# One wide product per weight tile in the feed-forward's first layer: 512 columns into a whole bank, the two half sums added by ScalarE and VectorE

## The reference, cut to what matters

```python
D_MODEL, SEQ, FFN_DIM, CONV_WIDTH = 1024, 256, 2752, 3

def conv_glu_ffn(h, w_in, conv_w, conv_b, w_out):
    S = h.shape[1]
    u = h @ w_in                                   # (256 x 1024) @ (1024 x 5504)
    up = jnp.pad(u, ((0, 0), (CONV_WIDTH - 1, 0), (0, 0)))
    c = conv_b
    for tap in range(CONV_WIDTH):
        c = c + up[:, tap:tap + S] * conv_w[tap]   # a causal filter of 3 taps along the tokens
    gate, val = c[..., :FFN_DIM], c[..., FFN_DIM:]
    return (jax.nn.silu(gate) * val) @ w_out       # (256 x 2752) @ (2752 x 1024)

# per layer:  x = x + attention(rmsnorm(x));  x = x + conv_glu_ffn(rmsnorm(x), ...)
```

## Time and profile before

| | us |
|---|---|
| median of 3 runs | 723.19 (720.53 to 723.85) |
| the profiled execution, its own time | 723.07 |
| its span in the profile | 721.3 |
| the two feed-forward loops within it | about 207 to 376 and 531 to 702 |

### The profile page before, as it was taken

One profiled execution on the slowest core, in us unless ns is written; L12 is line 12 of the kernel. 1 busy time (PEld: TensorE's weight loads), 2 busy tenths in 40 slices (PEclk: granted clock), 3 DMA queues, 4 the chain that ended last, 5 costly groups with the idle time before them and its releaser, 6 DMA issues.

```text
span 721.3 us, 11799 instructions
## 1 busy us (share of the span) xinstructions
PE 670.7 (93%) x4196; PEld 583.9 (81%) x4196; DVE 490.5 (68%) x922; ACT 394.9 (55%) x767; POOL 33.7 (5%) x61
## 2 busy tenths in 40 slices
PE   5999896999989999999999999787989999999995
PEld 4998565666889999999997788655889999999994
DVE  4387469684587777766678555685687777766675
ACT  5454334663585555555556455363685555555554
POOL 0200034000000000000000100302000000000000
PEclk9999998999999999999999999989999999999998
DMA  7465053000626544445541554420536545555521
GB/s 265 159 212 182 27 206 116 2 1 1 217 107 241 196 176 175 175 178 191 202 187 59 192 175 169 165 88 1 203 121 240 187 181 179 175 177 186 200 79 58
DMA packets 19614, 109.10 MB, mean 151 GB/s; under 512 B 2432, under 2 KB 2816, under 8 KB 10240
## 3 DMA queue, kind: packets, MB, share of 16 engines
q1 hardware_dynamic: 19584, 108.71, 41.9%
HBM read 107.65 MB, written 1.05 MB: 151 GB/s over the span
## 4 chain that ended last, share of the span: by engine, by line
PE 78%; DVE 12%; ACT 5%; DMA 2%; issue 2%; POOL 1%; SPq 0%; POOLq 0%; DVEq 0%; ACTq 0%
PE psA L356 11%; PE psA L357 11%; PE psA L358 11%; PE psT L452 6%; PE psO L454 6%; PE psO L453 6%; PE psO L452 6%; PE psT L454 6%; PE psT L453 6%; PE psO L641 2%; PE psO L617 2%; DVE stat L1461 2%; DMA stage<-in_w_group 2%; DVE win_lo L1227 2%; DVE arena L1495 1%
## 5 line engine op out<-in xcount | busy, mean ns | idle before, releaser
L1308 DVE TENSOR_TENSOR win_lo<-stage,win_hi 128x1024 fp32r<-128x1024 f32 x90 | 109.4, 1219 | 5.7 <-ACT win_hi L926 5.7
L1324 DVE SCALAR_TENSOR_TENSOR arena<-psO,prm,arena 128x255 f32<-128x255 f32 x84 | 40.1, 478 | 90.8 <-ACT arena L944 90.8
L926 ACT ACTIVATE win_hi<-stage 128x1024 fp32r<-128x1024 f32 x92 | 96.0, 1050 | 6.4 <-PE psA L358 6.4
L452 PE MATMUL psT<-hA_hi,win_hi 128*128 128x256 f32 x336 | 95.2, 283 | 1.7 <-DVE hA_lo L1243 1.7
L453 PE MATMUL psO<-hA_lo,win_hi 128*128 128x256 f32 x336 | 95.2, 283 | 0.0
L452 PE MATMUL psO<-hA_hi,win_hi 128*128 128x256 f32 x336 | 95.2, 283 | 0.0
L454 PE MATMUL psT<-hA_hi,win_lo 128*128 128x256 f32 x336 | 95.2, 283 | 0.0
L454 PE MATMUL psO<-hA_hi,win_lo 128*128 128x256 f32 x336 | 95.2, 283 | 0.0
L453 PE MATMUL psT<-hA_lo,win_hi 128*128 128x256 f32 x336 | 95.2, 283 | 0.0
L1227 DVE TENSOR_TENSOR win_lo<-stage,win_hi 128x1024 fp32r<-128x1024 f32 (+3 forms) x56 | 62.3, 1152 | 32.2 <-ACT win_hi L874 31.9
L944 ACT ACTIVATE arena<-psO,prm 128x256 f32<-128x256 f32 x42 | 23.7, 563 | 89.7 <-PE psO L454 89.7
(11 more groups left out here) (242 smaller groups left out, 1358.9 us busy)
## 6 DMA issues: line engine op xcount, KB each, us to landing
stage<-in_w_ffn_in SPq DMA_DIRECT2D x44, 1024.0 KB, 5.4
stage_out<-in_w_ffn_out SPq DMA_DIRECT2D x44, 516.0 KB, 3.5
stage<-in_w_kv SPq DMA_DIRECT2D x8, 1024.0 KB, 4.8
stage<-in_w_group SPq DMA_DIRECT2D x5, 1024.0 KB, 5.1
stage<-in_w_phi SPq DMA_DIRECT2D x4, 1024.0 KB, 4.9
stage<-in_w_nsa_out SPq DMA_DIRECT2D x4, 1024.0 KB, 5.0
stage<-in_w_dq SPq DMA_DIRECT2D x4, 1024.0 KB, 4.8
stage<-in_w_dout SPq DMA_DIRECT2D x4, 1024.0 KB, 4.8
```

Of the source, the lines that this page charges most:

```text
L452: mm(o, win_hi[:, slot, cs], hA_hi[:, k, :], start=k == 0, stop=False)
L926: act.activation(win_hi[:, slot, h * W // 2:(h + 1) * W // 2], stage[:, slot, h * W // 2:(h + 1) * W // 2], ACT.Copy).then_inc(sem["in_hi" ...
L1308: last = dve.tensor_tensor(win_lo[:, slot, cs], stage[:, slot, cs], win_hi[:, slot, cs].bitcast(F32), sub)
L1324: dve.scalar_tensor_tensor(conv[:, b, g, k:S], (psT, psO)[g][:, b, 0:S - k], prm[:, b, 4 * g + 2 - k:4 * g + 3 - k], conv[:, b, g, k:S], A ...
```

## The change

High and low half of the normalised tokens now lie side by side: one tile `hA` of [128, 8, 2, 256], of which `hA_hi` and `hA_lo` are views. `up` makes one product of 512 columns with the high weights (both halves as the moving operand, into a whole bank of 512) and one of 256 with the low weights, added to the first 256 columns of the bank. So u is in the bank as two sums: columns 0 to 255 hold high by high plus low by high, columns 256 to 511 hold high by low. ScalarE copies the second half into `u_part` in SBUF, and VectorE adds it to the first half of the bank and writes `u_sum`. The filter then reads `u_sum` instead of the bank, on both engines. VectorE now takes the gate's two taps first and then the value's, and copies the parameters ahead of the value's taps. ScalarE's first half split of `win` now stands between the copy and the filter of g = 1. TensorE's waits on `gate2` and `val2` become waits on `u_sum`.

```diff
--- before
+++ after
@@ tiles @@
-        hA_hi = sb("hA_hi", [P, KT, S], F32R)
-        hA_lo = sb("hA_lo", [P, KT, S], F32R)
+        hA = sb("hA", [P, KT, 2, S], F32R)
+        hA_hi, hA_lo = hA[:, :, 0, :], hA[:, :, 1, :]
+        u_part = arena[:, 4096:4608].rearrange("p (g q) -> p g q", g=2)
+        u_sum = arena[:, 4608:5120].rearrange("p (g q) -> p g q", g=2)
@@ TensorE, up(); up_last() in the same way @@
-                            o = (psT, psO)[g][:, b, 0:S]
-                            mm(o, win_hi[:, slot, cs], hA_hi[:, k, :], start=k == 0, stop=False)
-                            mm(o, win_hi[:, slot, cs], hA_lo[:, k, :], start=False, stop=False)
-                            last = mm(o, win_lo[:, slot, cs], hA_hi[:, k, :], start=False, stop=k == KT - 1)
+                            o = (psT, psO)[g][:, b, :]
+                            mm(o, win_hi[:, slot, cs], hA[:, k, :, :].rearrange("p a q -> p (a q)"), start=k == 0, stop=False)
+                            last = mm(o[:, 0:S], win_lo[:, slot, cs], hA_hi[:, k, :], start=False, stop=k == KT - 1)
@@ TensorE, the loop @@
-                        pe_.wait_ge(sem["val2"], 2 * i + (f0 + b + 1))
-                        pe_.wait_ge(sem["gate2"], 2 * i + (f0 + b + 1))
+                        pe_.wait_ge(sem["u_sum"], 4 * i + (2 * f0 + 2 * b + 2))
@@ ScalarE, step() @@
-                        act.activation(conv[:, b, g, :], (psT, psO)[g][:, b, 0:S], ACT.Identity,
+                        act.activation(u_part[:, g, :], (psT, psO)[g][:, b, S:2 * S], ACT.Copy).then_inc(sem["u_part"], 1)
+                        if g == 1 and split_next:
+                            split_in(j + 2, b, 0)
+                        act.wait_ge(sem["u_sum"], 2 * j + (2 * f0 + g + 1))
+                        act.activation(conv[:, b, g, :], u_sum[:, g, :], ACT.Identity,
                                        bias=prm[:, b, 4 * g + 3:4 * g + 4], scale=prm[:, b, 4 * g + 2:4 * g + 3]).then_inc(sem["conv0"], 1)
-                    if split_next:
-                        split_in(j + 2, b, 0)
@@ ScalarE, last_step() @@
-                    act.activation(conv[:, 1, 0, :], psT[:, 1, 0:S], ACT.Identity, bias=prm[:, 1, 3:4], scale=prm[:, 1, 2:3]).then_inc(sem["conv0"], 2)
+                    act.activation(u_part[:, 0, :], psT[:, 1, S:2 * S], ACT.Copy).then_inc(sem["u_part"], 2)
+                    act.wait_ge(sem["u_sum"], 2 * (f0 + NJ))
+                    act.activation(conv[:, 1, 0, :], u_sum[:, 0, :], ACT.Identity, bias=prm[:, 1, 3:4], scale=prm[:, 1, 2:3]).then_inc(sem["conv0"], 2)
@@ VectorE @@
+                def add_parts(j, b, g):
+                    dve.wait_ge(sem["u_part"], 2 * j + (2 * f0 + g + 1))
+                    dve.tensor_tensor(u_sum[:, g, :], (psT, psO)[g][:, b, 0:S], u_part[:, g, :], ALU.add).then_inc(sem["u_sum"], 1)
@@ VectorE, last_step() @@
+                    dve.wait_ge(sem["u_part"], 2 * (f0 + NJ))
+                    dve.tensor_tensor(u_sum[:, 0, :], psT[:, 1, 0:S], u_part[:, 0, :], ALU.add).then_inc(sem["u_sum"], 2)
+                    dve.wait_ge(sem["u_sum"], 2 * (f0 + NJ))
```

More of the change, by code:

```diff
@@ L106 @@
 scores smax negmax probs recip factor scaled_p pT_bank pT_act pT_dve oT_bank oT_hi oT_lo
-x_new u_bank conv0 gate1 val1 gate2 val2 silu prod a_hi a_lo
+x_new u_bank u_part u_sum conv0 gate1 val1 gate2 val2 silu prod a_hi a_lo
 dk_bank dk_act dk_dve dq_bank dq_act dq_dve
@@ L463, in up_last @@
                     pe_.wait_ge(sem["in_lo"], first + NJ)
-                    pe_.wait_ge(sem["gate2"], f0 + NJ - 2)
+                    pe_.wait_ge(sem["u_sum"], 2 * (f0 + NJ - 2))
                     for k in range(KT):
                         cs = slice(k * P, (k + 1) * P)
[L468 to L471, removed]
+                        o = psT[:, 1, :]
+                        before = mm(o, win_hi[:, slot, cs], hA[:, k, :, :].rearrange("p a q -> p (a q)"), start=k == 0, stop=False)
+                        last = mm(o[:, 0:S], win_lo[:, slot, cs], hA_hi[:, k, :], start=False, stop=k == KT - 1)
                     before.then_inc(sem["u_bank"], 1)
@@ L493, in ffn @@
                     for b in range(2):
-                        pe_.wait_ge(sem["val2"], 2 * i + (f0 + b + 1))
-                        pe_.wait_ge(sem["gate2"], 2 * i + (f0 + b + 1))
+                        pe_.wait_ge(sem["u_sum"], 4 * i + (2 * f0 + 2 * b + 2))
                         up(2 * i + (2 + b), b)
                         down(2 * i + (1 + b), 1 - b, False, False)
-                pe_.wait_ge(sem["val2"], f0 + NJ - 3)
-                pe_.wait_ge(sem["gate2"], f0 + NJ - 3)
+                pe_.wait_ge(sem["u_sum"], 2 * (f0 + NJ - 3))
                 up(NJ - 2, 0)
@@ L1323, in tap @@
                     wait()
-                    dve.scalar_tensor_tensor(conv[:, b, g, k:S], (psT, psO)[g][:, b, 0:S - k], prm[:, b, 4 * g + 2 - k:4 * g + 3 - k],
+                    dve.scalar_tensor_tensor(conv[:, b, g, k:S], u_sum[:, g, 0:S - k], prm[:, b, 4 * g + 2 - k:4 * g + 3 - k],
                                              conv[:, b, g, k:S], ALU.mult, ALU.add).then_inc(sem[done], 1)
+                def add_parts(j, b, g):
+                    dve.wait_ge(sem["u_part"], 2 * j + (2 * f0 + g + 1))
+                    dve.tensor_tensor(u_sum[:, g, :], (psT, psO)[g][:, b, 0:S], u_part[:, g, :], ALU.add).then_inc(sem["u_sum"], 1)
                 def step(j, b, split_next=True, split_wout=True):
+                    add_parts(j, b, 0)
                     tap(b, 0, 1, lambda: dve.wait_ge(sem["conv0"], 2 * j + (2 * f0 + 1)), "gate1")
+                    tap(b, 0, 2, lambda: dve.wait_ge(sem["gate1"], j + (f0 + 1)), "gate2")
+                    add_parts(j, b, 1)
+                    take_params(j + 1, 1 - b)
                     tap(b, 1, 1, lambda: dve.wait_ge(sem["conv0"], 2 * j + (2 * f0 + 2)), "val1")
-                    tap(b, 0, 2, lambda: dve.wait_ge(sem["gate1"], j + (f0 + 1)), "gate2")
                     tap(b, 1, 2, lambda: dve.wait_ge(sem["val1"], j + (f0 + 1)), "val2")
-                    take_params(j + 1, 1 - b)
                     if split_next:
@@ L1346, in last_step @@
                     taps = [prm[:, 1, k:k + 1] for k in range(2)]
+                    dve.wait_ge(sem["u_part"], 2 * (f0 + NJ))
+                    dve.tensor_tensor(u_sum[:, 0, :], psT[:, 1, 0:S], u_part[:, 0, :], ALU.add).then_inc(sem["u_sum"], 2)
+                    dve.wait_ge(sem["u_sum"], 2 * (f0 + NJ))
                     for k, done in ((1, "gate1"), (2, "gate2")):
                         dve.wait_ge(sem["conv0" if k == 1 else "gate1"], 2 * (f0 + NJ) if k == 1 else f0 + NJ)
-                        dve.scalar_tensor_tensor(conv[:, 1, 0, k:S], psT[:, 1, 0:S - k], taps[2 - k], conv[:, 1, 0, k:S],
+                        dve.scalar_tensor_tensor(conv[:, 1, 0, k:S], u_sum[:, 0, 0:S - k], taps[2 - k], conv[:, 1, 0, k:S],
                                                  ALU.mult, ALU.add).then_inc(sem[done], 1)
```

## The result

The changed kernel takes 723.98 us (median of 20 runs, 722.34 to 725.47) against 722.74 us before (20 runs, 720.53 to 723.94). The ratio is 1.0018, with a 95% interval of 1.0009 to 1.0026: slower by about 1.2 us. It lies within the 0.5% that was called "same" and within the range, but on the other side of no change than the forecast of 721.5.

The account below looks back on a forecast made before the run. TensorE was taken to bound the loop, at 8.30 us a group against VectorE's 8.22. The terms: 723.07 - 7.6 + 2 x 1.15 + 2.5 + 1.2 = 721.5 us, range 718.8 to 729.0.

Parts of the forecast that it names:

- What bounds the loop, the chain, its price: Feed-forward loop: TensorE sets the period at 8.30 us; VectorE's chain through ScalarE takes 8.09 to 8.22, 8.22 taken.
- The start term: Start of each layer: the first down waits for the longer elementwise chain of the first groups, +1.15 us a layer.
- The end terms: End of each layer: the last down waits for VectorE's longer chain, +2.5 us in layer 0, +1.2 in layer 1.
- The product term: Up in the loop: one product less per weight tile saves 13.6 ns a pair, 0.20 us a group, 7.6 in all.
- the clean stream: A down that no up precedes: 512-column products take 0.2264 us each, giving 0.346 a pair and 0.22 saved a group.
- The first: Loop: VectorE's chain exceeds 8.30 us and sets the period; 729 us at a chain of 8.40; chance 0.25.
- The second: Loop, starts and ends: VectorE's chain is only 8.01 us, so starts and ends cost less; 719.3 us; chance 0.15.
- The third: Up: the wide product pays back its saved cost; 727 us at 2.5 ns a product, 723 at 8 ns; chance 0.08.
- the fourth: Layer 0's last down: TensorE's clock falls in the 2.8 us gap, products take 0.427 us, 723.9 in all; chance 0.07.

Follow-up runs that it names:

- The doubled addition: The changed kernel with each VectorE addition preceded by the same addition into a tile nobody reads; 747.88 us, ratio 1.0346 to the kernel before.
- the kernel with grouped products: The changed kernel with each bank's 8 wide products first, then its 8 narrow ones (up_last still alternating); 721.01 us, ratio 0.9986 to the kernel before.
- both reordered ones: The changed kernel with wide products before narrow (721.01 us), and the same with the value bank as one wide, eight narrow, seven wide (720.97 us).

## Why the prediction was wrong, step by step

- **What bounds the loop, the chain, its price: right.** TensorE sets the loop, VectorE's chain takes 8.15 and 8.23 in turn, 8.19 on average (forecast 8.09 to 8.22, 8.22 taken). Addition 0.42, filter from SBUF 0.60, dependent taps 0.52: all as priced from rows of other lines. The doubled addition shows that a chain of 8.85 takes over.
- **The start term: right.** +1.10 and +1.09 against +1.15; removing it gave 11.48. The wait itself was 1.3 us and not 1.6, since TensorE, with less saved in up(0) and up(1), came later to it.
- **The end terms: right in kind, 0.33 us too high each** (+2.17 and +0.87 against +2.5 and +1.2). VectorE catches up by 8.39 - 8.19 = 0.20 a group, not by the 0.08 of the forecast, and so enters the last groups on time. Most of that comes from TensorE's longer period, not from a shorter chain. In layer 0 the last down but one waits too (0.33 us, at 381.45), which the forecast did not name; it costs nothing of its own, because the last down waits for VectorE's chain in any case.
- **The product term: this is the step that failed.** "I take 0.20, nearer to the clean stream" was -7.6 us; it measured 0.108 a group and -4.1 us, and with it the period was 8.39, not 8.30. Both prices of the pair were read from streams of one width. The trace of before held the sign that a wide product behind narrow ones costs more (0.03 us over 12 products of a down behind an up), and the forecast used it as a bound of 5 ns a product, then leaned to the other end. In the alternating order every wide product but the gate bank's first stands behind a narrow one: it takes 0.236 and the narrow one 0.117, 7 ns more for the pair than the forecast's 0.346. That term explains the miss: it is 3.5 us short, and the 0.8 us that starts and ends cost less than forecast could not make up for it. That the time still lay in the range is no merit of the mechanism: the two errors partly cancelled, and the range was 10 us wide.
- **The rivals.** The first did not take place in this kernel: in its loop no down waits. The second did not either, since the chain was 8.19 and not 8.01. The third had two sizes. At 2.5 ns a product it did not take place; at 8 ns, put at 723, it is what came nearest, with about 6.5 ns measured. The 2.5 ns are the rule of the Trainium skill, "TensorE: Matmul & The Clock Gate", section "Back-to-back issue gap", for the spacing of a single product. The rows of these runs show 6.5 ns for a product removed in the alternating order and 12 to 13 ns where the wide ones stand in runs (0.20 us a group for 16 products), so here the rule does not agree. In the fourth, the clock stayed at 1.00 over the gaps of the changed kernel (up to 2.10 us between starts; the 2.8 us of waiting in one piece that it supposed did not come); see below for a longer one.
- The sum set 7.6 us of gain against 6.0 us of cost and kept the difference, -1.6. An error of a fifth in the larger term was enough to turn its sign, and it was off by almost half.

## What to carry to other kernels

Price a merged instruction in the mix in which it will stand: the same product cost 0.226 or 0.236 us by its predecessor, and ordering like products in runs brought the group from 8.39 to the 8.30 of the forecast. An idle engine has room only for work that lies outside the chain which makes it wait: add up one round of the chain and compare it with the bound's period, not with its idle time. Where a trade is good in the middle of a pipeline and bad where it fills and drains, make it only in the middle; here that turned 0.2% lost into 1% won.

## What the runs showed of the hardware

A product of n columns with its own weight load took n/2.4 ns plus 13 ns in runs of one width, at 256 and 512 columns alike (0.120 and 0.2266 us), at the granted clock of 1.00. Behind narrow ones the first five wide products cost more: in the kernel with grouped products 0.233, 0.236, 0.228, 0.232 and 0.231 us, 27 ns too much together, and 0.2266 from the sixth on (means over the groups from 235 to 370 us, from the starts in the trace). The down of the kernel before shows the same series behind its narrow products, so it does not hang on this change. The first narrow product behind a wide one took 0.113 instead of 0.120. Why, the traces don't tell: the weight loads start, on average, within 0.01 us of the start of the product before, in the kernel before, the changed one and both reordered ones.

Behind a wait of TensorE the first two starts of a down were 0.34 us apart (386.21 and 386.55 above), 0.11 more than in a stream, and the next distances lay between 0.224 and 0.240 before they were back at 0.227, five to ten products on. So each wait cost TensorE a little more than its length.

TensorE's clock fell behind a gap of 3.69 us between starts, in the kernel with the doubled additions, at the last down but one of layer 0:

```profile
393.48 0.50 PE L359 MATMUL psA<-wout_hi,act_hi 128*128 128x512 f32 x1 [3.30 <-DVE act_lo L1352]
...
394.58 0.63 PE L359 MATMUL psA<-wout_hi,act_hi 128*128 128x512 f32 x1
395.00 0.63 PE L360 MATMUL psA<-wout_lo,act_hi 128*128 128x512 f32 x1
...
397.14 0.49 PE L359 MATMUL psA<-wout_hi,act_hi 128*128 128x512 f32 x1
397.47 0.40 PE L360 MATMUL psA<-wout_lo,act_hi 128*128 128x512 f32 x1
```

The busy time of that stretch, with the granted clock (us, then TensorE, weight loads, VectorE, ScalarE, GpSimd, the clock, DMA):

```profile
394.15:397.14 2.99, 2.99 (x9) 2.30 (x8) 2.25 (x5) 1.85 (x5) 0.00 (x0) 0.50 0.83 329
```

The first products start 0.34 and 0.33 apart, the first as behind any wait. From 394.15 to 397.14 they stand 0.427 apart at a granted clock of 0.50, which is 512 columns at the level of 1.2 GHz, and 0.33 and less after that. The surcharge of 13 ns is not to be seen at that level. So what the fourth rival supposed did not occur behind the gaps of the changed kernel (2.10 us at most, clock 1.00 from 381 to 386 us and on), and did behind this one.
